# Encoder layer on eight cores: norms, residual rows and the key, value and query steps in another order

## What is computed

```python
x = x + 0.5 * swiglu(rms_norm(x, ffn1_norm), ffn1_w_gate, ffn1_w_up, ffn1_w_down)
z = rms_norm(x, mix_norm) @ w_in
b_gate, c_gate, h, q_lat, kv_lat, k_rope_raw = jnp.split(z, cuts, axis=-1)
y_conv = short_conv_mixer(b_gate, c_gate, h, conv_w)     # b * conv3(c * h), 512 wide
y_att = latent_attention(q_lat, kv_lat, k_rope_raw, ...) # 8 heads, 64 + 32 wide, no mask
x = x + jnp.concatenate([y_conv, y_att], axis=-1) @ w_out
x = x + 0.5 * swiglu(rms_norm(x, ffn2_norm), ffn2_w_gate, ffn2_w_up, ffn2_w_down)
return rms_norm(x, final_norm)                           # meta tokens dropped
```

## Time and profile before

| | us |
|---|---|
| median of 3 runs | 4729.07 |
| lowest, highest | 4724.8, 5106.37 |
| the profiled execution, its own time | 4728.72 |
| its span (slowest core, core 6) | 4727.3 |
| spans of the 8 cores | 4712.4 to 4727.3 |
| FFN1, first to last down matmul | up to 1459 |
| mix phase | about 1459 to 2008 |
| attention | about 2031 to 3263 |
| FFN2 | 3291 to the end |

### The profile page before, as it was taken

The page is one execution under the profiler, slowest core; times in us unless marked ns, Lnnn a source line. Parts: engine busy times, 40 slices in busy tenths (PEclk is TensorE's granted clock), DMA queues, the critical chain, the costliest instruction groups (busy, mean ns, idle before and its releaser), DMA issues.

```text
span 4727.3 us, 78534 instructions; the slowest of 8 cores (4712.4 to 4727.3 us)
## 1 busy us (share of the span) xinstructions
PE 4526.8 (96%) x31256; PEld 2274.9 (48%) x31256; DVE 1236.3 (26%) x2190; ACT 2160.8 (46%) x3082; POOL 254.8 (5%) x441
## 2 busy tenths in 40 slices
PE   7999999999999999889999999898999999999999
PEld 3444444444444445455555555554444444444444
DVE  2222222222224554411111111223222222222222
ACT  2122222222214555499999999886222222222221
POOL 1000000000001221200000000000000000000000
PEclk9999999999999999999999999999999999999999
DMA  9533333333134554351111113315211111111110
GB/s 178 106 82 79 79 80 79 79 80 74 58 114 129 143 134 128 91 155 54 54 54 54 54 54 105 122 63 179 90 54 54 54 54 54 54 54 52 52 49 32
DMA packets 143799, 391.24 MB, mean 83 GB/s; under 512 B 21584, under 2 KB 44944, under 8 KB 142160
## 3 DMA queue, kind: packets, MB, share of 16 engines
q1 hardware_dynamic: 89952, 219.82, 14.7%
q0 software_dynamic: 51472, 159.72, 14.4%
q10 hardware_dynamic: 2016, 6.69, 0.4%
HBM read 318.42 MB, written 141.87 MB: 97 GB/s over the span
## 4 chain that ended last, share of the span: by engine, by line
PE 80%; ACT 8%; DMA 5%; DVE 4%; issue 3%; POOL 0%; ACTq 0%; DVEq 0%; POOLq 0%; SPq 0%
PE ps L309 18%; PE ps L312 18%; PE ps L382 16%; PE ps L1246 9%; ACT a_P L1253 7%; PE ps L779 5%; PE ps L1269 3%; PE tp L1193 3%; DMA f1wg<-ffn_w_gate 2%; PE ps L709 1%; PE ps L712 1%; PE tp L286 1%; DVE f2xn L277 1%; DMA x_d<-a_x 1%; ACT f2stmp L399 1%
## 5 line engine op out<-in xcount | busy, mean ns | idle before, releaser
L1253 ACT ACTIVATE a_P<-ps 128x1024 bf16<-128x1024 f32 x1280 | 1185.0, 1091 | 46.0 <-PE ps L1246 43.8
L1246 PE MATMUL ps<-a_QT,a_KT 112*128 112x512 bf16 x2560 | 777.1, 385 | 45.7 <-DMA a_V<-V_d 7.2
L1269 PEld LDWEIGHTS ps<-a_V,a_P 128*128 128x128 bf16 x10240 | 488.6, 98 | 307.6 <-issue 5.2
L1269 PE MATMUL ps<-a_V,a_P 128*128 128x65 bf16 x10240 | 526.0, 194 | 0.1
L309 PE MATMUL ps<-f1xnT,f1wg 128*128 128x512 bf16 x2112 | 500.4, 380 | 0.7 <-ACT f1xmT L293 0.7
L309 PE MATMUL ps<-f2xnT,f2wg 128*128 128x512 bf16 x2112 | 498.9, 379 | 1.4 <-ACT f2xnT L293 1.4
L312 PE MATMUL ps<-f1xnT,f1wu 128*128 128x512 bf16 x2112 | 498.9, 379 | 0.0
L312 PE MATMUL ps<-f2xnT,f2wu 128*128 128x512 bf16 x2112 | 498.9, 379 | 0.0
L327 ACT ACTIVATE f1stmp<-ps 128x512 f32<-128x512 f32 x264 | 157.6, 597 | 700.1 <-PE ps L312 700.0
L382 PE MATMUL ps<-f1wd,f1hT 128*128 128x512 bf16 x2112 | 470.4, 381 | 5.7 <-DMA f1wd<-ffn_w_down 4.1
L327 ACT ACTIVATE f2stmp<-ps 128x512 f32<-128x512 f32 x264 | 157.7, 597 | 693.2 <-PE ps L312 693.0
(11 more groups left out here) (162 smaller groups left out, 3085.2 us busy)
## 6 DMA issues: line engine op xcount, KB each, us to landing
f1res<-xin SPq DMA_DIRECT2D x50, 512.0 KB, 3.9
f2res<-x_d SPq DMA_DIRECT2D x50, 512.0 KB, 3.9
x_d<-f1res POOLq DMA_DIRECT2D x48, 512.0 KB, 3.2
m_xin<-x_d SPq DMA_DIRECT2D x48, 512.0 KB, 4.0
a_x<-x_d SPq DMA_DIRECT2D x12, 2048.0 KB, 10.3
x_d<-a_x POOLq DMA_DIRECT2D x12, 2048.0 KB, 9.1
y<-f2res POOLq DMA_DIRECT2D x48, 512.0 KB, 3.1
f1xin<-xin SPq DMA_DIRECT2D x46, 512.0 KB, 3.9
```

Of the source, the lines that this page charges most:

```text
L1246: ins = nc.tensor.matmul(sbank[:, j * 512:(j + 1) * 512], lhsT=KT[h][:, kt * 128:(kt + 1) * 128], rhs=QT[qc % 2][:, h, :], start=True, sto ...
L1253: ins = nc.scalar.activation(out=Pb[:, pi % NPB, :], in_=sbank, func=AF.Exp, scale=SCALE)
L1269: ins = nc.tensor.matmul(ob[:, qs, :], lhsT=Pb[:, pi % NPB, j * 512 + qs * 128:j * 512 + (qs + 1) * 128], rhs=V[h][:, kt0 + j, :], start=( ...
```

## The change

1. `ffn_phase`: `norm` of a tile's first rows is issued before the first group. For the other three, `norm(x + 1)` is issued in the middle of a group, behind `xpose(x)`, and thus ahead of the second half and of `finish`. The next load of the ring goes with it, ahead of `res_load`. FFN2's waits on `x2_d` are by 128 rows, and `wd` is waited for in pairs of pieces.
2. `attn_phase`: residual rows are stored and loaded in four DMAs of 128 rows (512 KB), each store behind the second half of its rows, each load behind the store of the same rows. The last tile's four `o_tr` are issued before FFN2's first two norms.
3. `mix_phase`: `qkv_step` is cut into `k_step`, `v_step`, `qr_step` and `qn_step`, whose bodies are as before. Group s of tile t issues step s of tile t - 1, behind `z_step` and ahead of `xnorm`. In tile 11 both query steps stand in group 2.

```diff
@@ ffn_phase
         for t in range(ntile):
             gate_up(t)
             hand = seam is not None and t == ntile - 1
+            if (t + 1, 0) in at:
+                norm(at[(t + 1, 0)], first_sq[0])
+                load_after(at[(t + 1, 0)] + R)
             for s in range(4):
...
                 res_load(cnt["SUB"] + 1)
-                if x is not None:
-                    norm(x, first_sq[0] if s == 0 else square(x))
...
                 down_half(t, s, 0, 128)
                 if x is not None:
-                    load_after(x + R)
                     xpose(x)
+                    if s < 3:
+                        norm(x + 1, square(x + 1))
+                        load_after(x + 1 + R)
...
                 down_half(t, s, 1, 128)
                 finish(r0, 128)
@@ mix_phase
                 g = z_step(t, s)
+                if t == 1 and s == 0:
+                    W(nc.tensor, s_wl[2], s_wl[2].n)
+                if 0 < t and (t < 11 or s < 3):
+                    (k_step, v_step, qr_step, qn_step)[s](t - 1)
+                if t == 11 and s == 2:
+                    qn_step(10)
                 nxt = s < tiles[t + 1][1]
                 if nxt:
                     xnorm(t + 1, s)
-                if s == 0 and t > 0:
-                    if t == 1:
-                        W(nc.tensor, s_wl[2], s_wl[2].n)
-                    qkv_step(t - 1)
@@ attn_phase
-    def load_x(tile):
+    def load_x(tile, s_):
         if tile >= 12:
             return
-        WT(nc.sync, ost.get(tile - 1))
-        s_xl.sig(nc.sync.dma_start(
-            out=x1, in_=T["x1_d"][tile * 512:(tile + 1) * 512, :].rearrange("(s p) d -> p s d", p=128)), 16)
+        if tile > 0:
+            WT(nc.sync, ost[tile - 1][s_])
+        r0 = tile * 512 + s_ * 128
+        s_xl[s_].sig(nc.sync.dma_start(out=x1[:, s_, :], in_=T["x1_d"][r0:r0 + 128, :]), 16)
...
-        if i == 7:
-            W(nc.gpsimd, s_or, 8 * (tile + 1))
-            ost[tile] = gq.dma(T["x2_d"][tile * 512:(tile + 1) * 512, :].rearrange("(s p) d -> p s d", p=128), x1)
+        if n2 == 1:
+            W(nc.gpsimd, s_or, 8 * tile + i + 1)
+            r0 = tile * 512 + s_ * 128
+            ost.setdefault(tile, []).append(gq.dma(T["x2_d"][r0:r0 + 128, :], x1[:, s_, :]))
...
-        steps.append((at + 10 + 8 * per, lambda: load_x(tile + 1)))
+        for s_ in range(4):
+            steps.append((at + 10 + (2 * s_ + 2) * per, lambda s_=s_: load_x(tile + 1, s_)))
...
-    next(ffn2)
     wob[:] = [ps[:, i, :] for i in range(4)]
...
     for a in range(4):
         o_tr(11, a)
+    next(ffn2)
```

More of the change, by code:

```diff
@@ L243, in load @@
             if a is not None:
-                for k in range(r0 // 512, (r0 + rows - 1) // 512 + 1):
-                    WT(nc.sync, a["x2"][k])
+                WT(nc.sync, a["x2"][r0 // 512][r0 % 512 // 128])
             ins = nc.sync.dma_start(out=place(x)[0:rows, :], in_=x_src[r0:r0 + rows, :])
@@ L441, in ffn_phase @@
             s_gu = [Sem(nc, tag + "gu%d" % j) for j in range(NJ)]
-            s_wd = [Sem(nc, tag + "wd%d" % j) for j in range(NJ)]
+            s_wd = [Sem(nc, tag + "wd%d" % j) for j in range(NJ // 2)]
             s_gB = Sem(nc, tag + "gB")
@@ L828, in fm_step, with k_step @@
                     ub_tok[t] = [a, gq.dma(bTd[:, :, row0:row0 + 512], bT[:, p, :, :])]
[L830 removed]
+        def k_step(t):
             p = t % 2
@@ L863, in qkv_step, with v_step @@
                                        KTn[o * 64:(o + 1) * 64, p, :, 0:ncol]))
+        def v_step(t):
+            p = t % 2
+            row0, nsub, ncol = tiles[t]
+            r = min(128, ncol)
             for tk in v_tok.get(t - 2, []):
@@ L878, in qkv_step, with qr_step @@
             after["kv"][t] = krd_tok[t] + k_tok[t] + v_tok[t]
[L879 to L899, removed]
+            qkv_end[t] = s_mm.n
+        def qr_step(t):
+            p = t % 2
+            row0 = tiles[t][0]
+            WT(nc.vector, tab_n[t])
+            for tk in q_tok.get(t - 2, []):
+                WT(nc.scalar, tk)
+                WT(nc.vector, tk)
+            for g in range(2):
+                for k in range(2):
                     i, b = bank()
+                    m = 4 + 2 * k + g
                     for c in range(3):
@@ L903, in qkv_step, with qn_step @@
                                                start=(c == 0), stop=(c == 2))
[L904 to L913, removed]
+                    W(nc.vector, s_mm, s_mm.sig(ins))
+                    bk_tok[i] = (s_ed, s_ed.sig(nc.vector.tensor_tensor(out=rt[:, g, k, :], in0=b,
+                                                                       in1=qcs[:, t % 3, k, :], op=ALU.mult)))
+                W(nc.vector, s_ed, s_ed.n)
+                rtok = (s_ed, s_ed.sig(nc.vector.tensor_tensor(out=QTr[:, p, g, :], in0=rt[:, g, 0, :],
+                                                              in1=rt[:, g, 1, :], op=ALU.add)))
+                W(nc.vector, s_ed, s_ed.n)
+            rope_tok[t] = rtok
+            q_tok[t] = []
+            WT(nc.gpsimd, rtok)
+            for o in range(4):
+                q_tok[t].append(gq.dma(T["QT_d"][o::4, 64:96, row0:row0 + 512].rearrange("h r c -> r h c"),
+                                       QTr[o * 32:(o + 1) * 32, p, :, :]))
+        def qn_step(t):
+            p = t % 2
+            row0 = tiles[t][0]
+            for m in range(4):
+                i, b = bank()
+                for c in range(3):
+                    ins = nc.tensor.matmul(b, lhsT=wuq[:, c, m * 128:(m + 1) * 128], rhs=qkT[:, p, c, :],
+                                           start=(c == 0), stop=(c == 2))
+                ntok = on_act(i, s_mm.sig(ins), QTn[:, p, m, :], b)
+            WT(nc.gpsimd, ntok)
+            for o in range(2):
+                q_tok[t].append(gq.dma(T["QT_d"][o::2, 0:64, row0:row0 + 512].rearrange("h r c -> r h c"),
+                                       QTn[o * 64:(o + 1) * 64, p, :, :]))
             qkv_end[t] = s_mm.n
@@ L999, in mix_phase @@
                     kr_rope(12)
-                    qkv_step(12)
+                    k_step(12)
+                    v_step(12)
                     yield
-        qkv_step(11)
+        k_step(11)
+        v_step(11)
+        qr_step(11)
+        qn_step(11)
         a_, b_ = flg[:, 0:1], flg[:, 1:2]
@@ L1085, in attn_phase @@
     s_ul = Sem(nc, "o_ul")
-    s_xl = Sem(nc, "o_xl")
+    s_xl = [Sem(nc, "o_xl%d" % i) for i in range(4)]
     s_oc = Sem(nc, "o_c")
@@ L1324, in attn_phase @@
         load_kv(0, h)
-    load_x(0)
+    for s_ in range(4):
+        load_x(0, s_)
     for tk in mx["pe"]:
```

13 lines of the change are left out of this document (7 added, 6 removed).

## The result

| | before, us | after, us |
|---|---|---|
| fastest execution | 4724.8 | 4679.17 |
| profiled execution, its span | 4728.72, 4727.3 (core 6) | 4679.17, 4677.7 (core 5) |
| spans of the 8 cores | 4712.4 to 4727.3 | 4672.8 to 4677.7 |
| ratio after / before | | 0.9899 (95%: 0.9857 to 0.9942) |

The changed kernel is 1.0% faster; the forecast was 4672 us, 1.2% less than before, and 4679.2 lies in the range of 4642 to 4700. In some executions of every kernel the cores of one die or of both ran at a lower granted clock and took longer; their times are left out, and where a kernel had only some cores at the full clock, the text names those.

The account below looks back on a forecast made before the run. The prediction took PE, busy for 96% of the span, as the bound, with time won only where it stands still. Its sum was 4728.7 - 41 - 20.5 - 8.4 + 13 = 4672 us, range 4642 to 4700.

Parts of the forecast that it names:

- part 4: Mix: spreading keys, values and queries over four groups makes PE wait longer for PSUM banks, +13 us.
- Part 1, -41: FFN2: norming the next rows before the final norm cuts 33 groups from 11.18 to 9.94 us, -41 us.
- The loop's cover: FFN2's one-place ring: issue, landing and norm take 7.4 us against 9.94; a landing up to 6.2 costs nothing.
- In FFN1 ... 0: FFN1: the same move of the norm finds no wait and no final norm, so it gains 0.
- the sentence on SP: FFN loads: SP issues the same loads with two kinds exchanged; the residual's has more than a group to land.
- Part 2, -20.5: Attention: storing and loading the residual by 128 rows removes the excess in query-tile pitch, -20.5 us.
- Part 3, -8.4 or -6.7: Seam to FFN2: earlier transposes and no residual wait, -8.4 us; -6.7 if the clock still falls.
- Eight matmuls at 0.425: Seam: eight matmuls at 0.425 instead of 0.216 cost 1.7 us, which goes if the shorter pause keeps the clock up.
- (a): Mix: the spread hides every bank wait; 4628 us, 2.1% faster; chance 0.14.
- (b): FFN2: loads of the one-place ring land late and transposes wait; 4763 us at a 9.0 us landing; chance 0.03.
- (c): FFN2: the early norm comes no earlier because something else holds ACT or DVE; 4713 us; chance 0.06.
- (d): Mix costs more as DVE's work slides from group to group; 4705 us at +3 us a tile; chance 0.09.

Follow-up runs that it names:

- e9: Changed kernel, residual stored by 128 rows but loaded by one 2 MB DMA per tile; attention with seam 1259.1 and 1258.6 us on cores 0 and 1.
- e3: Changed kernel with the V and query steps issued ahead of `z_step`, K's step left behind it; 4626.53 us.
- e8: Changed kernel, each FFN2 ring load preceded by the same 128-row load, whose landing SP awaits; FFN2 1456.8 to 1467.2 us on cores 4 to 7.
- e10: Kernel with V and query steps ahead of `z_step`, plus FFN1's second ring load and first residual load held until most down weights landed; 4634.74 us.
- e6: Kernel before, with only FFN2's first two norms moved behind the last tile's four transposes; attention with seam 1278.6 to 1281.7 us on cores 4 to 7.

## Where the prediction held, and the steps that failed

The step that failed is in part 4. Its sum counts only the time that PE waits, and puts the lower clock behind such a wait at nothing, without a reason, though parts 2 and 3 reckon with it. The waits came as forecast; the clock took 10.1 us on top, and mix cost 23.0 and not 13. Two smaller terms were off as well: FFN1's 0 was -4, and the excess in attention was read on the slowest core alone, 20.5 us where the median core has 15.

**Part 1, -41: right.** 9.94 us a group, -41.3, alone and in company. The loop's cover was right too: free with a short load ahead, used up with a long one. "In FFN1 ... 0" was wrong: -4 us. The step that failed is the sentence on SP, that the loads are only exchanged; I asked when the moved load is due, and not what it shares the DMA engines with where it used to stand.

**Part 2, -20.5: right on the core that it was read on, too large for the others.** The pitch came as read (65.75). The excess had been read on core 6, the slowest, as 20.5; the same three pitches give 13.6 to 18.0 on the other cores and 15 as the median, and alone the part measured -17.9, with the 2.1 us at the end of the seam in it, which I had booked under part 3. Core 6 itself went from 1281.6 to 1256.0 in attention, -25.6: the three pitches gave 20.7 and the seam 8.5, as forecast, but its first query tile took 3.4 us more, since PE waited 10.7 us instead of 7.2 for a load of values (`a_V`). That wait lies between 4.6 and 12.7 us over the cores of both kernels, so it is scatter and no term of the change.

The small transfers do cost more by themselves: four loads of 3.3 us (median to landing, kernel after) against one of 10.3. The rule on batches of 1 MiB or more that was weighed there (the Trainium skill, DMA: Bandwidth & Descriptors, Bandwidth) is true of the transfer and wrong as advice here: e9, which keeps the large load, is the slower one.

**Part 3, -8.4 or -6.7: as forecast on core 6's terms.** 5.27 became 1.01, a gain of 4.3 for 4.6 forecast; the 2.09 went with part 2, as said. "Eight matmuls at 0.425" did not go on core 5, so there the -6.7 holds; on cores 6 and 7 the first lots run at 0.86 us. From the last block to FFN2's first matmul core 6 gained 28.8 - 20.25 = 8.5 us, the median core 6.3.

**Part 4, +13: the sign and the waits right, the size not.** From K of one tile to K of the next, 1539.95 - 1494.54 = 45.41 us, against 44.24 before (1550.70 less 1506.46, the same matmuls a tile earlier): +1.17, the forecast to the hundredth. The brackets are shorter by 0.16 only because of where a row ends: a group with V's step is 1506.61 - 1494.54 = 12.07 us long, one without a step 8.19 (in both kernels), so V takes 3.88 us, for 3.90 worked out. The term that is missing is the clock: 6 x 1.69 = 10.1 us. I had charged a restart at a lower clock to the 7 us waits of attention and to the seam, and not to a wait of 2 us that I put there myself. 23.0 - 10.1 = 12.9 is left for the waits, against 13; core by core, with its own count of slow lots, it is 11.0 to 13.5.

**Rivals.** None came. (a), the spread that hides every bank wait, was given 0.14 and doesn't hold for the kernel after; e3 shows that its reasoning was sound but for the place: 519.2 is 30.0 below before, where I had put its bound at -31. The rule to rotate independent groups over banks (the Trainium skill, Perfetto Trace Analysis, Optimizing Tensor Performance) gives that time only when the evicting engine reaches the bank before its other work: with the same four banks the wait was 2.00 us behind `z_step` and none ahead of it. (b) needs about twice the landing that is seen; with two landings in the loop (e8) FFN2 is indeed slower than before, 1462 against 1436.5. Its price of (3.7 + landing - 9.94) for all 33 groups is too high, since a tile's first group is partly covered. (c) is refuted by the pitch. (d), mix at +46, didn't come either: the 10 us more than forecast are the clock's, and DVE's work slides nowhere, as the equal brackets of every tile show.

**The sum.** Core by median: -4.3 + 23.0 - 21.5 - 41.3 = -44; forecast 0 + 13 - 28.9 - 41 = -57. The slowest core, which sets the time, moved by 49.6, since it was core 6 with its long waits before and is one like the others now. That the slowest core comes within 7 us of the forecast, and the median core only within 13, owes something to luck: the slowest core before had the longest waits in attention, and FFN1's 4 us, not foreseen, stand against part of the 10 that mix cost on top. And the sentence that a measurement tells about 2% (95 us) from no change took the noise too large: the interval of the ratio, 0.9857 to 0.9942, leaves no change outside, and the executions at the full clock took 4724.4 to 4729.8 us before and 4679.17 and 4679.34 after.

## What to carry to other kernels

Where engines work through fixed orders, a bank is free when its evictor reaches it, so place a matmul group by what that evictor has just been given: the same steps cost 23 us behind `z_step` and won 30 ahead of it. Ask of every wait that is left or added inside a matmul stream whether the clock falls behind it; here 2.0 us did it in half of the cases, 1.1 in none. Read excesses on several cores, not on the slowest alone, and when a load moves away from a place, look at what it leaves there.

## What the runs showed that I had not expected

- The granted clock fell behind some of many equal waits: 6 of 11 at 2.00 us (7 on one core), for 1.69 us each. What tells the 6 from the 5 wasn't found.
- With 512 KB less in the first 110 us, where the DMA engines are full, tile 1's first down matmul came 3.2 us sooner, a thing that no row of waits names.
- In e10 two cores of one die started with a granted clock of 0.81, at a PE that was busy 99% of the time and with no wait for a load, and so did two cores each in e6, e8 and e9. No run here tells why.
- A seam that waits for two things gains nothing from the removal of the first (e6: 5.3 to 1.0, and from at most 2.3 to 4.9 and more).
